# A transformer stack on one core: branch products placed between the steps of a differential attention, and weight slabs rounded on ScalarE

## What is computed

```python
def diff_attention(q, k, v, lam):
    s = jnp.einsum('bqahd,bkahd->bahqk', q, k).astype(jnp.float32) * (B_QK_DIM ** -0.5)
    p = jax.nn.softmax(s, axis=-1)
    a = (p[:, 0] - lam * p[:, 1]).astype(v.dtype)
    return jnp.einsum('bhqk,bkhe->bqhe', a, v)
...
    m = g_a * (y_a @ wa) + g_b * (y_b @ wb) + g_c * (y_c @ wc)
    return m @ wo
```

## Time and profile before

| | |
|---|---|
| median of three runs | 4189.26 us |
| the profiled execution: its own time | 4195.7 us |
| its span, first to last instruction | 4193.9 us |
| TensorE busy | 3679.0 us (88%) |
| VectorE busy | 1701.1 us (41%) |
| ScalarE busy | 996.7 us (24%) |
| GpSimd busy | 2027.0 us (48%) |
| TensorE's granted clock, mean | 0.921 |
| DRAM traffic | 389.23 MB, mean 93 GB/s |

### The profile page before, as it was taken

The page is one execution under the profiler, slowest core; times in us unless marked ns, Lnnn a source line. Parts: engine busy times, 40 slices in busy tenths (PEclk is TensorE's granted clock), DMA queues, the critical chain, the costliest instruction groups (busy, mean ns, idle before and its releaser), DMA issues.

```text
span 4193.9 us, 45719 instructions
## 1 busy us (share of the span) xinstructions
PE 3679.0 (88%) x18162; PEld 2924.1 (70%) x18162; DVE 1701.1 (41%) x2845; ACT 996.7 (24%) x1988; POOL 2027.0 (48%) x1216
## 2 busy tenths in 40 slices
PE   7787689778878999799767999999999669999999
PEld 5665378667754787577655887787668457886887
DVE  5844434343344644355464111432272661113330
ACT  1033321353323101212253001221121451012210
POOL 5352078658641565374301665565555005564655
PEclk9886599888987999899889999999999889999999
DMA  6621034233421554142100222232322002232322
GB/s 219 209 88 63 12 127 137 89 92 120 150 62 55 191 169 137 50 160 72 51 1 21 96 93 88 84 92 91 110 71 81 1 1 86 88 98 78 93 93 93
DMA packets 109862, 389.23 MB, mean 93 GB/s; under 512 B 12057, under 2 KB 16537, under 8 KB 108242
## 3 DMA queue, kind: packets, MB, share of 16 engines
q1 hardware_dynamic: 89280, 315.11, 23.4%
q10 hardware_dynamic: 20370, 71.20, 5.0%
HBM read 379.93 MB, written 6.32 MB: 92 GB/s over the span
## 4 chain that ended last, share of the span: by engine, by line
PE 78%; DVE 12%; ACT 6%; issue 2%; POOL 2%; DMA 1%; ACTq 0%; SPq 0%; DVEq 0%
PE ps L287 20%; PE ps L288 20%; PE ps L289 20%; PE ps L1349 3%; ACT diff_p L1397 2%; DVE small_d L1405 2%; PE ps L854 2%; PE ps L374 2%; PE ps L376 2%; PE ps L375 2%; PE ps L1044 1%; POOL wlo L2274 1%; DVE ps L896 1%; PE ps L1065 1%; DVE ps L884 1%
## 5 line engine op out<-in xcount | busy, mean ns | idle before, releaser
L2272 POOL CAST whi<-raw 128x1024 fp32r<-128x1024 f32 (+1 forms) x606 | 621.2, 1025 | 2105.6 <-DMA raw<-in_w 2105.1
L2274 POOL TENSOR_TENSOR wlo<-raw,whi 128x1024 fp32r<-128x1024 f32 (+1 forms) x606 | 1418.0, 2340 | 48.5
L287 PE MATMUL ps<-hhi,whi 128*128 128x512 f32 x2056 | 839.3, 408 | 65.3 <-DVE hlo L903 34.0
L288 PE MATMUL ps<-hlo,whi 128*128 128x512 f32 x2056 | 820.8, 399 | 0.0
L289 PE MATMUL ps<-hhi,wlo 128*128 128x512 f32 x2056 | 819.7, 399 | 0.0
L287 PEld LDWEIGHTS ps<-hhi,whi 128*128 128x128 f32 x2056 | 390.8, 190 | 185.7 <-issue 62.1
L288 PEld LDWEIGHTS ps<-hlo,whi 128*128 128x128 f32 x2056 | 391.5, 190 | 96.9 <-issue 6.7
L289 PEld LDWEIGHTS ps<-hhi,wlo 128*128 128x128 f32 x2056 | 391.2, 190 | 95.2
L287 PE MATMUL ps<-chi,whi 128*128 128x256 f32 x864 | 262.4, 304 | 61.3 <-DVE fc_sum L597 42.5
L288 PE MATMUL ps<-clo,whi 128*128 128x256 f32 x864 | 252.8, 293 | 0.0
L289 PE MATMUL ps<-chi,wlo 128*128 128x256 f32 x864 | 252.1, 292 | 0.0
(11 more groups left out here) (371 smaller groups left out, 6637.5 us busy)
## 6 DMA issues: line engine op xcount, KB each, us to landing
raw<-in_w SPq DMA_DIRECT2D x574, 512.0 KB, 3.5
ada<-in_ada ACTq DMA_DIRECT2D x96, 512.0 KB, 4.4
raw<-in_w SPq DMA_DIRECT2D x16, 384.0 KB, 3.2
att_toe<-toe_dram ACTq DMA_DIRECT2D x12, 256.0 KB, 3.7
raw<-in_w SPq DMA_DIRECT2D x16, 192.0 KB, 2.3
x<-in_x SPq DMA_DIRECT2D x4, 512.0 KB, 9.3
cond<-in_cc ACTq DMA_DIRECT2D x2, 1024.0 KB, 5.0
kc_dram<-kc ACTq DMA_DIRECT2D x2, 1024.0 KB, 4.2
```

The costliest lines, as they stand in the source:

```text
L287: nc.tensor.matmul(o, whi[:, buf, c], hi[:, k, 0:n], start=(k == 0), stop=False)
L288: nc.tensor.matmul(o, whi[:, buf, c], lo[:, k, 0:n], start=False, stop=False)
L2272: nc.gpsimd.tensor_copy(whi[:, buf, 0:c], raw[:, buf, 0:c]).then_inc(slab_hi, 1)
L2274: nc.gpsimd.tensor_tensor(wlo[:, buf, 0:c], raw[:, buf, 0:c], whi[:, buf, 0:c].bitcast(F32), ALU.subtract).then_inc(slab_split, 1)
```

## The change

Three things change together.

- The attention's units are handled closer together: the transposes of unit t-1 and the product of t-2 stand in step t, the eviction of t-3, the square of t-4. Each map has its own maximum, negative and exponentials. The second map's exponentials are written over its scores in PSUM; the fold reads them there, in the same step, and the scores of t wait for the fold of t-1. The six buffers for probabilities become four.
- Branch a, the conv products and branch c are woven between the steps of attention and HeadNorm. `weave` goes by size: a step counts 1 (`Part.size`), an output tile of a `Branch` kt/8 (the second `size` in the diff). All other weavings use the same rule.
- `whi` is made by ScalarE. The pass for slab n stands in ScalarE's order before the step that first uses slab n-3 (`AHEAD`). GpSimd keeps the subtraction.

The constant columns for the shift of the first map go as well.

```diff
 RING = 5
+AHEAD = 3
 EPS = 1e-6
...
         def new_slab(row, blocks):
             slab_row.append(row)
+            slab_step.append(len(order))
             slab_cols.append(blocks * P)
...
         def weave(main, filler):
 
-            at_ = 0
+            size = [part.size(i) for part, i in filler]
+            at_, behind = 0, 0
             for n, (part, i) in enumerate(main):
                 place(part, i)
-                upto = (n + 1) * len(filler) // len(main)
-                for other, j in filler[at_:upto]:
-                    place(other, j)
-                at_ = upto
+                while at_ < len(filler) and behind + size[at_] / 2 <= (n + 1) * sum(size) / len(main):
+                    place(*filler[at_])
+                    behind += size[at_]
+                    at_ += 1
+            for other, j in filler[at_:]:
+                place(other, j)
 
         class Part:
             steps = 1
 
             def begin(self):
                 pass
+
+            def size(self, i):
+                return 1
...
+            def size(self, i):
+                return self.kt / KT if i % 2 else 1
...
-                self.steps = self.N + 5
+                self.steps = self.N + 4
...
             def place(self, t):
+                if 1 <= t < self.N + 1:
+                    self.turned.append((new_tile([]), new_tile([])))
                 if 2 <= t < self.N + 2:
-                    self.turned.append((new_tile([]), new_tile([])))
-                if 3 <= t < self.N + 3:
                     self.tile.append(new_tile([]))
...
                     if t:
-                        pe.wait_ge(self.ex, self.ex0 + 2 * t)
+                        pe.wait_ge(self.pn, self.pn0 + t)
...
-                u = t - 2
+                u = t - 1
                 if 0 <= u < self.N:
                     pe.wait_ge(self.pn, self.pn0 + u + 1)
...
-                u = t - 3
+                u = t - 2
                 if 0 <= u < self.N:
                     h, i = self.units[u]
...
-                u = t - 5
+                u = t - 4
                 if 0 <= u < self.N:
                     act.wait_ge(self.cl, self.cl0 + u + 1)
...
-                    act.wait_ge(self.nm, self.nm0 + t + 1)
-                    if t >= 2:
-                        act.wait_ge(tile_done, self.turned[t - 2][1] + 1)
                     for a in range(2):
-                        nc.scalar.activation((self.p1 if a else self.p0)[t % 2], pb(2 + 2 * a, TT), ACT.Exp, scale=SCALE,
+                        act.wait_ge(self.nm, self.nm0 + 2 * t + a + 1)
+                        if a == 0 and t >= 2:
+                            act.wait_ge(tile_done, self.turned[t - 2][1] + 1)
+                        nc.scalar.activation(pb(4, TT) if a else self.p0[t % 2], pb(2 + 2 * a, TT), ACT.Exp, scale=SCALE,
                                              bias=self.neg_at[t % 2][:, a:a + 1],
                                              accum_out=self.den_at[t % 2][:, a:a + 1]).then_inc(self.ex, 1)
...
             def vector(self, dve, t):
                 if t < self.N:
+                    small = self.max_at[t % 2], self.neg_at[t % 2]
                     dve.wait_ge(self.s, self.s0 + 2 * t + 2)
                     for a in range(2):
-                        nc.vector.tensor_reduce(self.max_at[t % 2][:, a:a + 1], pb(2 + 2 * a, TT), AX_X, ALU.max)\
+                        nc.vector.tensor_reduce(small[0][:, a:a + 1], pb(2 + 2 * a, TT), AX_X, ALU.max)\
                             .then_inc(self.mx, 1)
-                    dve.wait_ge(self.mx, self.mx0 + 2 * t + 2)
-
-                    nc.vector.scalar_tensor_tensor(self.neg_at[t % 2], self.max_at[t % 2], -SCALE,
-                                                   cst[:, SHIFT0:SHIFT0 + 2], ALU.mult, ALU.add).then_inc(self.nm, 1)
-                u = t - 1
-                if 0 <= u < self.N:
-                    den, rec = self.den_at[u % 2], self.rec_at[u % 8]
-                    p0 = self.p0[u % 2]
-                    dve.wait_ge(self.ex, self.ex0 + 2 * u + 2)
-                    nc.vector.reciprocal(rec, den).then_inc(self.rd, 1)
-                    dve.wait_ge(self.rd, self.rd0 + 2 * u + 1)
-                    nc.vector.scalar_tensor_tensor(self.fold_at[u % 2], den[:, 0:1], neglam[:, self.l:self.l + 1],
-                                                   rec[:, 1:2], ALU.mult, ALU.mult).then_inc(self.rd, 1)
-                    dve.wait_ge(self.rd, self.rd0 + 2 * u + 2)
-                    nc.vector.scalar_tensor_tensor(p0, self.p1[u % 2], self.fold_at[u % 2], p0, ALU.mult, ALU.add)\
-                        .then_inc(self.pn, 1)
-                u = t - 4
+
+                        dve.wait_ge(self.mx, self.mx0 + 2 * t + a + 1)
+                        nc.vector.tensor_scalar(small[1][:, a:a + 1], small[0][:, a:a + 1], -SCALE,
+                                                0.0 if a else -10.0 * math.log(2.0), ALU.mult, ALU.add)\
+                            .then_inc(self.nm, 1)
+                u = t - 3
                 if 0 <= u < self.N:
                     tile, y = self.tile[u], self.y(u)
                     dve.wait_ge(tile_done, tile + 1)
...
+                if t < self.N:
+                    den, rec, p0 = self.den_at[t % 2], self.rec_at[t % 8], self.p0[t % 2]
+                    dve.wait_ge(self.ex, self.ex0 + 2 * t + 2)
+                    nc.vector.reciprocal(rec, den).then_inc(self.rd, 1)
+                    dve.wait_ge(self.rd, self.rd0 + 2 * t + 1)
+                    nc.vector.tensor_scalar(self.fold_at[t % 2], den[:, 0:1], neglam[:, self.l:self.l + 1], rec[:, 1:2],
+                                            ALU.mult, ALU.mult).then_inc(self.rd, 1)
+                    dve.wait_ge(self.rd, self.rd0 + 2 * t + 2)
+                    nc.vector.scalar_tensor_tensor(p0, pb(4, TT), self.fold_at[t % 2], p0, ALU.mult, ALU.add)\
+                        .then_inc(self.pn, 1)
...
-            START = 12
+            START = 11
...
-            for part, i in main:
-                place(part, i)
-            run(L["a"], L["conv"], L["c"])
+            weave(main, steps(L["a"], L["conv"], L["c"]))
             run(L["b"])
...
+        class SlabHi(Part):
+
+
+            def scalar(self, act, n):
+                buf, c = n % RING, slab_cols[n]
+                act.wait_ge(raw_loaded[buf], 16 * (n // RING + 1))
+                nc.scalar.activation(whi[:, buf, 0:c], raw[:, buf, 0:c], ACT.Copy).then_inc(slab_hi, 1)
+
+        round_slab = SlabHi()
+        planned, order[:] = list(order), []
+        rounded = 0
+        for at_, step in enumerate(planned):
+            while rounded < len(slab_row) and slab_step[max(rounded - AHEAD, 0)] <= at_:
+                order.append((round_slab, rounded))
+                rounded += 1
+            order.append(step)
...
             for n in range(len(slab_row)):
                 buf, c = n % RING, slab_cols[n]
-                pool.wait_ge(raw_loaded[buf], 16 * (n // RING + 1))
-                nc.gpsimd.tensor_copy(whi[:, buf, 0:c], raw[:, buf, 0:c]).then_inc(slab_hi, 1)
                 pool.wait_ge(slab_hi, n + 1)
```

More of the change, by code:

```diff
@@ L64 @@
 IDENT, SWAP, BLOCK = 0, P, 2 * P
-EPS_COL, EPS_SMALL, ONE_COL, R1024, R256, R128, SHIFT0, SHIFT1 = range(3 * P, 3 * P + 8)
-N_CST = 3 * P + 8
+EPS_COL, EPS_SMALL, ONE_COL, R1024, R256, R128 = range(3 * P, 3 * P + 6)
+N_CST = 3 * P + 6
 class Tally:
@@ L185, in program @@
         slab_row = []
+        slab_step = []
         slab_cols = []
@@ L1314, in begin @@
                 self.mx, self.mx0 = take("diff_max", 2 * n)
-                self.nm, self.nm0 = take("diff_negmax", n)
+                self.nm, self.nm0 = take("diff_negmax", 2 * n)
                 self.ex, self.ex0 = take("diff_exp", 2 * n)
@@ L2129, in program @@
         sqs = [zone(f"sq{i}", [P, T], 156 + 2 * i)[:, :] for i in range(2)]
-        dp = [zone(f"diff_p{i}", [P, TT], 150 + 3 * i)[:, :] for i in range(6)]
+        dp = [zone(f"diff_p{i}", [P, TT], 150 + 3 * i)[:, :] for i in range(4)]
         dsq = [zone(f"diff_sq{i}", [P, P], 168 + i / 2)[:, :] for i in range(2)]
```

9 lines of the change are left out of this document (4 added, 5 removed).

## The result

The changed kernel takes 4246.45 us (median of 4 runs, 4240.55 to 4249.72) beside 4192.52 for the kernel before on the same chip: ratio 1.0121, 95% interval 1.0105 to 1.0137. It is slower by 1.2%. Its profiled execution has a span of 4238.5 us, the one before 4193.9; the 44.6 us between them are what follows.

What follows compares the result with a forecast made beforehand. TensorE holds 78% of the chain; attention and branches run one after the other. Terms -41 - 6 + 35 + 13 + 11 + 6 - 10 = +8 on the profiled 4195.7 give 4204, 4197 in median terms; range 4105 to 4260 us.

Steps and rivals of the forecast that it cites:

- The likeliest case: Whole kernel: gain and stalls cancel, within 21 us of the kernel before, 4168 to 4210 us; chance 0.4.
- the side that had 0.3: Whole kernel: the outcome slower than the kernel before, beyond the 21 us a measurement can tell; chance 0.3.
- Attention and branches: Second block, both layers: weaving gives 409 us a layer, -41 us; SGU tiles a step earlier, -6 us.
- the four bare steps: Attention steps with no full filler behind them: scores wait for the fold, 1.1 us each, one 3.4; 7 us.
- My 320 us: TensorE's own work per layer in the woven stretch: attention 115, fillers 202, HeadNorm's transposes 3 us.
- The down products: `f_down0`: ScalarE's square stands behind a pass awaiting its load, seven stalls of 5.0 us, +35; clock, +13.
- The start: Before the first projection: ScalarE's first passes stand behind two Silu, start moves from 36.0 to 47.3 us, +11.
- Token-major values: Value groups with two slabs each: ScalarE waits about 6 us for loads at a group's start; +6 us (0 to 20).
- The mixed stage: Softmax and stick-breaking with the context's products: GpSimd needs less per slab, -10 us (bounds -45 and +35).
- my rival with a price of 43: Mixed stage: ScalarE's passes keep epilogues or exponentials behind landings, 4250 us; chance 0.3 shared with more attention clock loss.
- the attention fills well: Attention: bank waits half of those counted and the clock stays up, 4111 us; chance 0.2 for anything to 4168.
- The slower rival: ScalarE holds up the mixed stage, 4250 us, or more clock loss in the attention, 4253 us; chance 0.3 together.

Runs made afterwards that it cites:

- experiment 6: The changed kernel with VectorE's eviction and clamp ahead of the two maxima and slab rounding back on GpSimd: 4038.4 us, ratio 0.9628.
- Experiment 4: The changed kernel with VectorE's eviction and clamp placed first in its step, ahead of the two maxima: 4104.87 us, ratio 0.9796.
- experiment 5: The changed kernel with slabs rounded two ahead instead of three, and the first passes right behind the first norm: 4182.45 us, ratio 0.9979.
- experiment 1: The changed kernel with slab rounding back on GpSimd, new attention step and weave kept: 4183.91 us, ratio 0.9981.
- Experiment 2: The kernel before with only the rounding moved to ScalarE, three slabs ahead; attention and weave as before: 4276.01 us, ratio 1.0200.
- Experiment 8: The kernel before with only VectorE's eviction and clamp moved ahead of the maxima: 4157.81 us, ratio 0.9919.
- experiment 9: The kernel before with branch products woven between the steps of its own attention, weave by size, rounding on GpSimd: 4359.11 us, ratio 1.0389.

## Why the prediction was right and wrong

The likeliest case, no change within 0.5%, did not come: the kernel is 1.2% slower, on the side that had 0.3, and inside the range. The sum was +8 on the profiled execution, and the traces show +44.6. Term by term:

**Attention and branches, forecast -41 and -6, measured -11.5. This is the term that failed.** The parts under it held one by one: 26 waits a layer counted, 26 found; 60 us for the products' and the transposes' waits computed, 60.1 measured; the fold's bound on the scores 7 us with the four bare steps, 2.6 found in layer 0; the fold from PSUM 1.02 us, as from SBUF; the gate's wait of 3.5 us down to 1.0. All idle time in layer 0 is 66 us where 77 were forecast.

What was mis-sized is the clock. I put it at 12 us a layer between bounds of 0 and 40. Forecast without it, a stretch was 397; measured it was 427.3 and 420.6, which leaves 30 and 24 us net. Set against the forecast's own busy time the gap is wider: 361 us where the sum had 320, partly hidden by the 11 us of idle time that I had too much. Some 8 of these 41 us are the sum itself, since experiment 6 is busy for 334.1 us at clock 0.99 with the first matmuls of b (about 328 without). Experiment 4 shows the rest from the other side: with the same matmuls and the waits gone, TensorE's busy time falls by 31 us in layer 0 alone. I had argued that waits under 3.07 us, 9 to 14 us apart, would cost less than the one that I had seen. Each did: they were 2.3 us long on average (up to 3.5) and cost 1.2 us of matmul time each, where that one cost 2.8. But the 12 us allowed them 0.5 each.

From the first scores to b TensorE is busy 361.6 us in the kernel before, at a mean clock of 0.91, and 366.5 in the changed one at the same 0.91, for the same matmuls: the change saved no matmul time at all, only idle time (76.6 to 66.4 us). My 320 us supposed that weaving brings the clock with it. The 0.83 in the earlier trace rows, in a stretch with 77 us of idle time and six such waits among it, was the warning: with 26 of them the clock stayed at 0.91, and with the eviction's waits gone it was 0.98.

**The down products, +35 and +13, measured +52.4, nearly right, and by the mechanism named.** Seven waits, 33.3 us together (forecast 5.0 each, 4.8 found), and 19 for the rest. TensorE's busy time from first to last norm sum is 19 us longer than in experiment 5 (118.2 against 99.15), at a granted clock of 0.85 against 1.00. So each wait cost 2.7 us behind it rather than 1.9. As to the rule of the Trainium skill ("TensorE: Matmul & The Clock Gate", "HAM oscillation — how this bites in real kernels") that waiting on a DMA once per tile pays the slow start at every tile, the trace agrees: the two sums behind each of the seven waits run at the lower level, 2.08 us together where they took 1.02. Experiments 1 and 5 show the cause; in this stage the latter differs by one slab of distance only.

**The start, +11, measured +11.3**, first projection at 47.3 as computed from the earlier trace rows. That nothing covers it was right as well.

**Token-major values, +6, measured +9.6** (4.1 and 5.5), but elsewhere than I put it. The first stage lost nothing (162.7 us from first projection to first softmax scores before, 161.3 after); the second block's groups did, where ScalarE holds the gate's work behind landings: in layer 1 TensorE waits 5.2 us for the gate's low half (`ab_lo`), 0.6 in experiment 1. Experiment 2 has 6.5 and 7.2.

**The mixed stage, -10 and 0 for the weave by size, measured -17.4**, of the right sign and inside the bounds, but with luck. I put it down to GpSimd's relief alone. Experiment 2 has that relief with the weave by count and wins nothing (1207.7 us), experiment 1 has the weave by size alone and wins nothing (1206.6); it takes both. And a single trace of this stage is good to some 10 us. That ScalarE would hold the stage up, my rival with a price of 43, is refuted: every kernel with ScalarE's rounding and the weave by size is fastest there.

**The rivals.** That the attention fills well was wrong for this kernel, but what it asked for, the waits gone and the clock up, is experiment 4's single edit. The slower rival named two causes; the second, more clock loss in the attention, is the one that came, with 30 of its 56 us. And a reading in the first part was too quick: with TensorE waiting mostly on exponentials, I took L1369's six waits in the earlier trace rows as evidence of a cost to come. Experiment 8 shows that the late eviction was already worth 34 us.

## What to carry to other kernels

When work is woven into a loop with shared banks, look for the instruction that frees a bank and put it first in its engine's step: here 0.34 us of VectorE work behind 2 us of maxima (and in the old step the fold) cost 34 us unwoven and 142 to 312 us woven, some four tenths of that through the clock (31 of 74 us in the one layer taken apart). A pass that waits for a DMA belongs on an engine with nothing urgent behind it, or late enough in the order that the load has landed; "three ahead" on a tile of three slabs waits for a load that is issued only when the tile ends, and two ahead cost nothing in the down products. Where GpSimd works beside VectorE, an input left in PSUM can be worth more than it looks: the old step's fold takes 3.2 us instead of 1.02 there, the new one does not. Measure parts of a change apart: of these three, rounding on ScalarE lost 2% alone, the new step lost 1.3% alone, and weaving on the old step lost 4% or won 2.7%, depending on one instruction's place.

## What the runs showed of the hardware

VectorE's fold stretches beside a GpSimd operation when both its inputs are in SBUF, and does not when one of them is in PSUM. The old step's fold (128x768, both maps in SBUF) takes 1.02 us in the 42 units of experiment 9 in which GpSimd is idle and 3.18 to 3.19 in 21 of the 22 others. The new step's fold, the same operation with the second map in PSUM, takes 1.02 us in every unit, 24 of 32 in each layer of the changed kernel beside GpSimd's subtract. The operations of the tables in experiment 5, both inputs in SBUF too, fit: a 1x64 operation took 0.21 us just before GpSimd's 128x1024 subtract began and 2.36 while it ran, about the length of one subtract (2.34), and a 1x2 operation took 1.95. In the kernel before, with GpSimd idle at that point, they took 0.21 and 0.15. So does VectorE's busy time in the mixed stage, 553 us with GpSimd busy 654 and 509 with GpSimd busy 489, with the same instructions (1037). What the two engines share, no run shows.

A wait costs well over its own length: the kernel with the eviction first won 43 us of idle time in layer 0 and 31 us of matmul time with it, at a granted clock of 0.98 instead of 0.91.
